# Delta heads: row broadcasts of the queries' decays issued behind the replicated reads of the diagonal blocks

## The chip, the core and the metric

The kernel runs on one core of a Trainium2 chip. The metric is the time on the device in microseconds (us), from the core's first to its last instruction and what lies around that; the median of the runs is compared. A core has a matrix engine (TensorE, in the profile PE, with its weight loads as PEld), VectorE (DVE), ScalarE (ACT), GpSimd (POOL) and SyncE (SP), which here issues all DMAs. Each engine works through its own list of instructions in order, and waits on semaphores for the others and for DMAs.

## The reference

One inference step of a small diffusion backbone of two layers, for a prompt of 128 tokens and a latent sequence of 1024, both with 1024 features. Layer 0 mixes a gated linear recurrence with windowed attention, layer 1 is a bidirectional gated DeltaNet with 8 heads; each layer ends in a SwiGLU network. The change lies in the DeltaNet. Cut to what matters, for one head and one direction, with chunks of tokens:

```python
decay = exp(where(incl, gc[:, None] - gc[None, :], NEG))       # gc: running sum of g in a chunk
a_mat = where(strict, beta[:, None] * kk * decay, 0.0) + eye(C)
sol   = triangular_solve(a_mat, concat([v * beta, k * (beta * exp(gc))]))   # u, w
qk    = (q @ k.T) * decay
qg    = q * exp(gc)[:, None]
for each chunk, in order:                                      # S starts from the context's state
    v_new = u - w @ S
    o     = qg @ S + qk @ v_new
    S     = S * exp(gc[-1]) + kd.T @ v_new
```

`exp(gc)` of the last factor of `qg` is what the moved DMAs bring: one number for each token, needed by every one of the 128 features. The outputs are the two sequences, the keys and values, and the final states of the recurrences.

## The kernel before

The 1152 tokens (9 blocks of 128) lie along the free dimension, features along the 128 partitions. The DeltaNet stage (`delta_stage`) takes the 8 heads one after another; for all engines but TensorE the heads 1 to 6 are a hardware loop (`heads`), and the first and the last head are written apart. Nothing but the order of the lines decides the order of the work: each engine's function lists its instructions, and semaphores tie the engines together. In the traced execution the stage runs from about 1615 to 2838 us.

One head goes as follows. TensorE projects v and z (`tile`), and in the scan the next head's k and q (`ahead`); VectorE and ScalarE convolve and normalise. `blocks_of` (lines 2441 to 2450, VectorE) makes the strictly triangular matrices of both directions, and by a reduction (L2448) the 16 x 16 blocks on their diagonals, `dn.part[d]`. The inverse of these blocks is found by substitution (`substitute`, L1797), for which each partition needs the block's rows in its own free dimension. SyncE brings them there through DRAM: two copies of `dn.part[d]` into `blocks_dram` (`blocks_spill` in the trace, L1869), a wait until they have landed (`a_out`), and one read that spreads each of the 16 rows there over 8 partitions, `dn.rep[d]` (L1871, the replicated read). VectorE substitutes direction 0, GpSimd direction 1; `expand` (L1815) then writes the inverses of the blocks into full matrices, `tt[0]` (`dn_tt`) and `tt[1]` (which lies in the buffer of `osum`, the previous head's output). TensorE transposes them (`turn_of`, L2107) and builds the full inverse from 16 to 128 in three levels (`x_of`, `d_of`, L2119 to L2137), with masked blocks that GpSimd makes (`masked`). Then come the solution, and the scan over the blocks in both directions.

SyncE's function (`body`, from L1854) lists for each head, in this order: the two loads of the states; the two row broadcasts of `exp(gc)` into `dn.qg[d]` (`rows`, L1847: 128 partitions x 9 blocks x 128 numbers from `rows_dram`, `rows_spill` in the trace); the copies and replicated reads of both directions; the store of the previous head's output to `y_dram` (`y_spill`, L1877); the loads of weight panels, each behind a wait for a split of GpSimd; the next head's broadcasts for the decay matrix; and the stores of the final states. The head starts when TensorE has issued the last output of the previous one (`o_full`). All these DMAs go through one queue, q1 of the profile.

`dn.qg[d]` is read by GpSimd's `decayed_q(d)`, which waits for the states and both broadcasts (`s_loaded` at 64 a head) and stands behind the second masked block of direction 1. The store of `osum` is waited for (`y_stored`) by VectorE, before it expands direction 1 into that buffer, and by ScalarE before the first output.

Of the kernel before, what the change touches and what calls it, by code (L numbers as in the profile page):

```python
# [1732 lines left out]
def delta_stage(s, dn, back):  # L1733
# [11 lines left out]
    with ExitStack() as ctx:  # L1745
        def sem(name):
            return ctx.enter_context(nc.semaphore("dn_" + name))
# [16 lines left out]
        s_loaded, ws_full, vn_ready, sn_full, s_ready, o_full, o_act, o_dve = (  # L1764
            sem(n) for n in ("s_loaded", "ws_full", "vn_ready", "sn_full", "s_ready", "o_full", "o_act", "o_dve"))
# [8 lines left out]
        def by_block(t):  # L1774
            return t[:].rearrange("p (n w) -> p n w", w=P)
# [51 lines left out]
        def heads(eng, body):  # L1827

            body(0, True, True)
            with eng.Fori(1, LAST) as h:  # L1830
                body(h, False, True)
            body(LAST, False, False)
# [5 lines left out]
        @block.sync  # L1838
        def _(sp):
            def load(h, j):  # L1840
                s.sp_load(sp, 4 * h + (p0 + j), (p0 + j) % 2)

            by_head = s.rows_dram.rearrange("q (n h) c -> q h n c", h=DN_H)

            def rows(h, q, to):

                return sp.dma_start(by_block(to), by_head[q, ds(h, 1)].to_broadcast([P, NT, P]))  # L1847

            sp.sem_inc(fin_stored, 32)
            sp.sem_inc(y_stored, 16)  # L1850
            for d in range(2):
                rows(0, d, dn.rows[d]).then_inc(rows_full, 16)
            for j in range(2, 6):
                load(0, j)  # L1854

            def body(h, first, more):
                if not first:
                    sp.wait_ge(o_full, 17 * h)
                for d in range(2):
                    sp.dma_start(dn.state[d][0][:], I["state_delta"][d, ds(h, 1)].rearrange("a p n -> p (a n)")  # L1860
                                 ).then_inc(s_loaded, 16)
                for d in range(2):
                    rows(h, 2 + d, dn.qg[d]).then_inc(s_loaded, 16)

                for d in range(2):
                    sp.wait_ge(wt_ready, 6 * h + (3 * d + 2))
                    copies = s.blocks_dram[d].rearrange("(b r) (m x) -> r b m x", r=2, m=BASE)
                    for r in range(2):
                        sp.dma_start(copies[r], dn.part[d][:].rearrange("p n c -> p (n c)")).then_inc(a_out[d], 16)  # L1869
                    sp.wait_ge(a_out[d], 32 * h + 32)  # L1870
                    sp.dma_start(dn.rep[d][:].rearrange("p m n c -> p (m n c)"),  # L1871
                                 s.blocks_dram[d].rearrange("b (o x) -> b o x", o=1
                                                            ).to_broadcast([2 * NK, BASE // 2, NT * BASE * BASE])
                                 ).then_inc(rep_full[d], 16)
                if not first:
                    sp.wait_ge(y_done, h)
                    sp.dma_start(s.y_dram[:, ds(h - 1, 1), :].rearrange("p a t -> p (a t)"), dn.osum[:]  # L1877
                                 ).then_inc(y_stored, 16)
                if more:
                    load(h, 6)  # L1880
                    load(h, 7)
                    sp.wait_ge(qg_ready, 2 * h + 2)
                    sp.wait_ge(u_full, 2 * h + 2)
                    for d in range(2):
                        rows(h + 1, d, dn.rows[d]).then_inc(rows_full, 16)
                else:

                    sp.wait_ge(s.panel_used.sem, p0 + 4 * DN_H)
                    sp.wait_ge(y_stored, 16 * DN_H)
                    sp.dma_start(s.hl[:, 0:LAST, :].bitcast(F32), s.y_dram).then_inc(back.landed, 16)  # L1890
                sp.wait_ge(fin_ready, 2 * h + 2)
                for d in range(2):
                    sp.dma_start(s.O["delta"][ds(h, 1), d].rearrange("a p n -> p (a n)"), dn.fin[d]
                                 ).then_inc(fin_stored, 16)
                if more:
                    load(h, 8)
                    load(h, 9)
            heads(sp, body)
            sp.wait_ge(fin_stored, 32 * DN_H + 32)

# [826 lines left out]
```

## Time and profile before

| what | value |
|---|---|
| median of the runs | 3823.32 us (3822.99 to 3826.45, 3 runs) |
| the profiled execution | 3837.11 us, span 3835.3 us |
| TensorE busy | 3357.6 us, 88% of the span |
| VectorE, ScalarE, GpSimd busy | 50%, 27%, 30% |
| granted clock of TensorE, mean | 0.942 of full speed |
| queue q1 | 103372 packets, 234.82 MB, 19.6% of the 16 engines' span |

The table is an average over stages with different limits: the projections and the SwiGLU networks keep TensorE full, while in the DeltaNet heads the engines wait for one another. What a wait is worth is read in its own stage. In the rows below, a timeline's columns are the start in us, the duration in us, the engine, the line of the kernel, the operation and its tiles, the count, and in brackets the engine's idle time before it and what ended that. For a DMA the duration is that of its issue; when it landed is in a view of its own.

### The profile page before, as it was taken

The page shows a single profiled execution, that of the slowest core. Times are in us where ns is not written, and L with a number is a line of the kernel's source. Part 1 is how long each engine was busy: PE and PEld are TensorE (multiplying, and loading weights), DVE is VectorE, ACT ScalarE, POOL GpSimd, SP SyncE. Part 2 cuts the span into 40 slices and gives each one's busy share as a digit, 9 for nine tenths or more (in the row PEclk, how much of TensorE's full clock was granted, in tenths as well). Part 3 has the DMA queues.
Part 4 walks back from the last instruction along what each step waited for, and adds up shares of the span by engine and source line. Part 5 has one row for each costly group of instructions (what it writes and reads, how often), then busy time and mean ns, then how long its engine had stood idle before and what let it go on. Part 6 is the DMA issues. An engine that isn't in the chain of part 4 may idle for free. (4 is left out here: it accounts for less than half of the span.)

```text
span 3835.3 us, 51814 instructions
## 1 busy us (share of the span) xinstructions
PE 3357.6 (88%) x20310; PEld 3203.7 (84%) x20310; DVE 1925.0 (50%) x2759; ACT 1031.7 (27%) x1573; POOL 1139.3 (30%) x797
## 2 busy tenths in 40 slices
PE   3984799899999999588888789788888999999996
PEld 2972589799999999478778778788788999999995
DVE  8758654734433445655465554655646132222227
ACT  3227340311111111343333433433422211111110
POOL 2213001321221112263554535535532212112121
PEclk8987799999999999799999899899999999999998
DMA  4420101212112211231221221222310111111111
GB/s 162 181 98 8 57 7 39 88 69 80 66 61 77 73 67 61 74 71 41 61 64 30 64 71 31 65 56 47 98 74 32 39 45 44 40 44 45 39 45 66
DMA packets 103577, 237.92 MB, mean 62 GB/s; under 512 B 8108, under 2 KB 61132, under 8 KB 100428
## 3 DMA queue, kind: packets, MB, share of 16 engines
q1 hardware_dynamic: 103372, 234.82, 19.6%
q8 instruction: 173, 2.83, 0.3%
q14 instruction: 32, 0.26, 0.0%
HBM read 217.54 MB, written 17.26 MB: 61 GB/s over the span
## 5 line engine op out<-in xcount | busy, mean ns | idle before, releaser
L55 PE MATMUL psum<-h_high,panel_high 128*128 128x384 f32 x3624 | 1246.0, 344 | 113.1 <-DVE h_low L495 81.1
L56 PE MATMUL psum<-h_low,panel_high 128*128 128x384 f32 x3624 | 1223.9, 338 | 0.0
L57 PE MATMUL psum<-h_high,panel_low 128*128 128x384 f32 x3624 | 1223.1, 337 | 0.0
L187 POOL TENSOR_TENSOR panel_low<-panel_raw,panel_high 128x1024 fp32r<-128x1024 f32 x196 | 488.0, 2490 | 1716.2 <-ACT panel_high L182 1673.4
L55 PEld LDWEIGHTS psum<-h_high,panel_high 128*128 128x128 f32 x3624 | 690.9, 191 | 154.4 <-issue 92.9
L56 PEld LDWEIGHTS psum<-h_low,panel_high 128*128 128x128 f32 x3624 | 691.5, 191 | 0.0
L57 PEld LDWEIGHTS psum<-h_high,panel_low 128*128 128x128 f32 x3624 | 690.0, 190 | 0.0
L847 DVE TENSOR_TENSOR ffn_product<-ffn_silu_gate,psum 128x1152 f32<-128x1152 f32 x44 | 59.6, 1354 | 712.4 <-PE psum L57 711.1
L182 ACT ACTIVATE panel_high<-panel_raw 128x1024 fp32r<-128x1024 f32 x195 | 205.1, 1052 | 627.6 <-PE psum L57 560.5
L55 PE MATMUL psum<-ffn_mid_high,panel_high 128*128 128x384 f32 x1056 | 355.2, 336 | 12.5 <-DVE x L650 7.5
L57 PE MATMUL psum<-ffn_mid_high,panel_low 128*128 128x384 f32 x1056 | 354.3, 336 | 0.0
L56 PE MATMUL psum<-ffn_mid_low,panel_high 128*128 128x384 f32 x1056 | 354.1, 335 | 0.0
L647 DVE SCALAR_TENSOR_TENSOR x<-psum,mod,x 128x128 f32<-128x128 f32 x192 | 67.3, 350 | 318.2 <-PE psum L57 306.8
L55 PEld LDWEIGHTS psum<-ffn_mid_high,panel_high 128*128 128x128 f32 x1056 | 199.4, 189 | 16.2 <-DVE x L650 8.8
L56 PEld LDWEIGHTS psum<-ffn_mid_low,panel_high 128*128 128x128 f32 x1056 | 199.2, 189 | 0.0
L57 PEld LDWEIGHTS psum<-ffn_mid_high,panel_low 128*128 128x128 f32 x1056 | 199.2, 189 | 0.0
L650 DVE SCALAR_TENSOR_TENSOR x<-psum,mod,x 128x768 f32<-128x768 f32 x192 | 193.5, 1008 | 0.0
L236 DVE CUSTOM_DVE_ANT_0 psum<-ffn_mod_panels,ffn_cond_rows 128x1024 f32<-128x1024 f32 x96 | 143.0, 1490 | 98.8 <-DMA ffn_mod_panels<-in_wmod 95.0
L772 ACT ACTIVATE ffn_mid_high<-ffn_product 128x1152 fp32r<-128x1152 f32 x44 | 51.5, 1169 | 512.1 <-DVE ffn_product L847 512.1
L769 ACT ACTIVATE ffn_silu_gate<-psum 128x1152 f32<-128x1152 f32 x44 | 49.9, 1135 | 439.5 <-PE psum L57 439.5
L236 DVE CUSTOM_DVE_ANT_0 psum<-in_mod_panels,in_cond_rows 128x1024 f32<-128x1024 f32 x64 | 99.0, 1547 | 47.7 <-DMA in_mod_panels<-in_wmod 44.9
L2307 ACT ACTIVATE dn_raw_k<-psum 128x384 f32<-128x384 f32 x144 | 70.3, 488 | 102.6 <-PE psum L2119 102.6
(320 smaller groups left out, 4740.5 us busy)
## 6 DMA issues: line engine op xcount, KB each, us to landing
panel_raw<-in_stream SPq DMA_DIRECT2D x197, 512.0 KB, 3.3
ffn_mod_panels<-in_wmod SPq DMA_DIRECT2D x24, 1024.0 KB, 7.3
dn_rep<-blocks_spill SPq DMA_DIRECT2D x16, 1152.0 KB, 7.7
in_mod_panels<-in_wmod SPq DMA_DIRECT2D x16, 1024.0 KB, 5.8
dn_qg<-rows_spill SPq DMA_DIRECT2D x16, 576.0 KB, 14.4
first_mod_panels<-in_wmod SPq DMA_DIRECT2D x8, 1024.0 KB, 14.0
x<-in_x SPq DMA_DIRECT2D x3, 1536.0 KB, 14.3
x<-in_x SPq DMA_DIRECT2D x1, 4608.0 KB, 15.9
```

What stands on the lines that cost most here:

```text
L55: pe.matmul(out, wh, xh, start=first, stop=False)
L56: pe.matmul(out, wh, xl, start=False, stop=False)
L57: return pe.matmul(out, wl, xh, start=False, stop=last)
L182: act.activation(self.wh[buf][:], self.raw[buf][:], ACT.Copy).then_inc(self.split_high.sem, 1)
L187: pool.tensor_tensor(self.wl[buf][:], self.raw[buf][:], self.wh[buf][:].bitcast(F32), ALU.subtract).then_inc(self.split_low.sem, 1)
L236: s.nc.vector.tensor_tensor_reduce(out=s.psum[:, 6:8, :], in0=panels[:, a, :].rearrange("p (b w) -> p b w", b=2), in1=rows[:, m, :].rearra ...
L647: dve.scalar_tensor_tensor(xf[:, 0:TP], s.psum[:, b0, 0:TP], g[0], xf[:, 0:TP], ALU.mult, ALU.add)
L650: return dve.scalar_tensor_tensor(later, s.psum[:, b0 + 1:b0 + 3, 0:TW], g[1], later, ALU.mult, ALU.add)
L769: act.activation(tiled(silu[:]), banks(s, 0), ACT.Silu).then_inc(s.gate_ready.sem, 1)
L772: act.activation(mid_h[slot][:], prod[:], ACT.Copy).then_inc(s.mid_high.sem, 1)
L847: dve.tensor_tensor(tiled(prod[:]), tiled(silu[:]), banks(s, 1), ALU.mult).then_inc(s.prod_ready.sem, 1)
L2307: act.activation(dn.xl[n % 2], psum[:, 6 + use % 2, 0:TW], ACT.Copy).then_inc(xb_read, 1)
```

## The change

The two lines that issue the row broadcasts move, within one head, from behind the state loads to behind the second replicated read, ahead of the store of the previous head's output. What is transferred, the semaphores and all waits stay.

```diff
--- before.py
+++ after.py
@@ -1860,9 +1860,6 @@
                     sp.dma_start(dn.state[d][0][:], I["state_delta"][d, ds(h, 1)].rearrange("a p n -> p (a n)")
                                  ).then_inc(s_loaded, 16)
                 for d in range(2):
-                    rows(h, 2 + d, dn.qg[d]).then_inc(s_loaded, 16)
-
-                for d in range(2):
                     sp.wait_ge(wt_ready, 6 * h + (3 * d + 2))
                     copies = s.blocks_dram[d].rearrange("(b r) (m x) -> r b m x", r=2, m=BASE)
                     for r in range(2):
@@ -1872,6 +1869,8 @@
                                  s.blocks_dram[d].rearrange("b (o x) -> b o x", o=1
                                                             ).to_broadcast([2 * NK, BASE // 2, NT * BASE * BASE])
                                  ).then_inc(rep_full[d], 16)
+                for d in range(2):
+                    rows(h, 2 + d, dn.qg[d]).then_inc(s_loaded, 16)
                 if not first:
                     sp.wait_ge(y_done, h)
                     sp.dma_start(s.y_dram[:, ds(h - 1, 1), :].rearrange("p a t -> p (a t)"), dn.osum[:]
```

SyncE's list in the first head, with the lines taken out (-) and put in (+); line numbers behind the change are lower by three. `dn_part` are the diagonal blocks (6746 direction 0, 6747 direction 1), `dn_rep` their replicated form:

```order
 L1860 DMA dn_state_6750<-in_state_delta 128x128
+L1866 DMA blocks_spill<-dn_part_6746 8x16x144 x2
+L1868 DMA dn_rep_6734<-blocks_spill 128x1x2304
+L1866 DMA blocks_spill<-dn_part_6747 8x16x144 x2
+L1868 DMA dn_rep_6735<-blocks_spill 128x1x2304
 L1847 DMA dn_qg_6727<-rows_spill 128x9x128
 L1847 DMA dn_qg_6728<-rows_spill 128x9x128
-L1869 DMA blocks_spill<-dn_part_6746 8x16x144 x2
-L1871 DMA dn_rep_6734<-blocks_spill 128x1x2304
-L1869 DMA blocks_spill<-dn_part_6747 8x16x144 x2
-L1871 DMA dn_rep_6735<-blocks_spill 128x1x2304
```

The copies of direction 0 now follow the state loads directly, and the broadcasts stand between the second replicated read and the loads of weight panels. The first head has no store of an earlier output.

SyncE's list in the loop over the heads 1 to 6 before the change, from the first replicated read on, with the waits; `dn_osum` is the previous head's output:

```order
L1871 DMA dn_rep_6734<-blocks_spill 128x1x2304 [waits dn_a_out0]
L1866 REGISTER_ALU
L1869 DMA blocks_spill<-dn_part_6747 8x16x144 [waits dn_wt_ready]
L1869 DMA blocks_spill<-dn_part_6747 8x16x144
L1871 DMA dn_rep_6735<-blocks_spill 128x1x2304 [waits dn_a_out1]
L1877 ISA [waits dn_y_done]
L1877 DMA y_spill<-dn_osum 128x1152
```

The same place after it:

```order
L1868 DMA dn_rep_6734<-blocks_spill 128x1x2304 [waits dn_a_out0]
L1863 REGISTER_ALU
L1866 DMA blocks_spill<-dn_part_6747 8x16x144 [waits dn_wt_ready]
L1866 DMA blocks_spill<-dn_part_6747 8x16x144
L1868 DMA dn_rep_6735<-blocks_spill 128x1x2304 [waits dn_a_out1]
L1847 ISA
L1847 DMA dn_qg_6727<-rows_spill 128x9x128
L1847 ISA
L1847 DMA dn_qg_6728<-rows_spill 128x9x128
L1876 ISA [waits dn_y_done]
L1876 DMA y_spill<-dn_osum 128x1152
```

The store of the output came directly behind the second replicated read; now the two broadcasts are issued between them. The waits in front of the copies, the reads and the store are the same.

## Rows read from the trace of the kernel before

**Rows 1.** Which engine waited for what, delta stage, 1640 to 2830 us.

```profile
engine line waited for: us in total, times, longest us
POOL dn_inverse L1803 <- DMA dn_rep<-blocks_spill: 119.3, 8, 17.0
PE psum L2107 <- DVE dn_tt L1818: 79.3, 8, 11.7
DVE dn_inverse L1803 <- DMA dn_rep<-blocks_spill: 73.5, 8, 9.8
```

**Rows 2.** Timeline of TensorE, end of the third head's projection and first transposes.

```profile
start us, us, engine line op out<-in xcount [idle before <-releaser]
...
1985.75 0.34 PE L57 MATMUL psum<-h_high,panel_low 128*128 128x384 f32 x1
1995.47 2.45 PE L2107 MATMUL psum<-ident,dn_tt 128*128 128x128 f32 x9 [9.38 <-DVE dn_tt L1818]
```

**Rows 3.** Timeline of VectorE in the third head (same columns).

```profile
...
1973.93 2.54 DVE L2434 RECIPROCAL dn_kd<-dn_kd 96x384 f32<-96x384 f32 x1
1985.64 0.31 DVE L1803 TENSOR_TENSOR dn_inverse<-dn_unit_blocks 128x144 f32<-128x144 f32 x1 [9.17 <-DMA dn_rep<-blocks_spill]
...
1994.05 1.36 DVE L1818 TENSOR_TENSOR dn_tt<-dn_inverse,dn_diagonal_blocks 128x1152 f32<-128x1152 f32 x1
...
2011.19 1.35 DVE L1818 TENSOR_TENSOR dn_osum<-dn_inverse,dn_diagonal_blocks 128x1152 f32<-128x1152 f32 x1
```

**Rows 4.** Timeline of SyncE in the third head (same columns); SPq issues DMAs.

```profile
...
1958.65 0.85 SPq L1860 DMA_DIRECT2D dn_state<-in_state_delta  x2
1959.70 1.34 SPq L1847 DMA_DIRECT2D dn_qg<-rows_spill  x2
1966.41 3.57 SPq L1869 DMA_DIRECT2D blocks_spill<-dn_part  x2
1978.01 0.58 SPq L1871 DMA_DIRECT2D dn_rep<-blocks_spill  x1
1978.71 1.21 SPq L1869 DMA_DIRECT2D blocks_spill<-dn_part  x2
1986.51 0.57 SPq L1871 DMA_DIRECT2D dn_rep<-blocks_spill  x1
1987.29 0.42 SPq L1877 DMA_DIRECT2D y_spill<-dn_osum  x1
...
2108.68 0.86 SPq L1860 DMA_DIRECT2D dn_state<-in_state_delta  x2
```

**Rows 5.** DMA issues, single broadcasts first, then medians of the stage.

```profile
issues: line engine op xcount, KB each, median us to landing
dn_qg<-rows_spill SPq DMA_DIRECT2D x1, 576.0 KB, 11.6
dn_qg<-rows_spill SPq DMA_DIRECT2D x1, 576.0 KB, 17.1
...
dn_rep<-blocks_spill SPq DMA_DIRECT2D x16, 1152.0 KB, 7.7
y_spill<-dn_osum SPq DMA_DIRECT2D x7, 576.0 KB, 8.2
dn_state<-in_state_delta SPq DMA_DIRECT2D x16, 64.0 KB, 2.8
```

**Rows 6.** Rate that the DMAs moved, 1958 to 1998 us in 40 slices.

```profile
...
GB/s 70 332 221 126 80 74 68 59 35 70 66 72 89 89 83 79 81 143 126 36 0 147 295 249 194 258 86 98 0 101 221 258 203 240 171 300 277 0 0 0
```

**Rows 7.** Timeline of SyncE at the end of the decay stage.

```profile
1611.51 0.39 SPq L1597 DMA_DIRECT2D rows_spill<-decay_rows_of_sums  x1
1614.23 0.41 SPq L1847 DMA_DIRECT2D dn_qn<-rows_spill  x1
```

**Rows 8.** Timeline of GpSimd in the third head.

```profile
...
1994.26 1.44 POOL L1803 TENSOR_TENSOR dn_inverse<-dn_unit_blocks 128x144 f32<-128x144 f32 x1 [14.69 <-DMA dn_rep<-blocks_spill]
...
2014.16 2.64 POOL L1906 TENSOR_TENSOR dn_qg<-dn_qn,dn_qg 128x1152 f32<-128x1152 f32 x1
```

**Rows 9.** Busy time by stretch, third head; PEclk is the granted clock.

```profile
core 0: us, PE busy (x) PEld busy (x) DVE busy (x) ACT busy (x) POOL busy (x), PEclk, DMA share, GB/s
1982.00:1986.00 4.00, 4.00 (x24) 3.77 (x22) 0.33 (x2) 0.00 (x0) 0.00 (x0) 1.00 0.72 159
1994.00:1998.00 4.00, 2.50 (x10) 1.99 (x11) 2.65 (x3) 1.03 (x3) 3.35 (x6) 0.50 0.17 69
1998.00:2002.00 4.00, 4.00 (x24) 4.00 (x24) 0.00 (x0) 1.43 (x3) 3.37 (x9) 0.62 0.00 0
```

## The prediction

> **What bounds the kernel now.** I read the waits of the delta stage first (1640 to 2830 us), then one head of it (the third, 1958 to 2109 us) on the matrix engine, VectorE, SyncE and GpSimd, then the landing times of its DMAs. The eight heads run one behind another, so what one head loses is lost eight times. In [rows 1] TensorE waits 79.3 us in eight times for `dn_tt` of line 1818: the expanded inverse of the diagonal blocks of direction 0. VectorE, which makes that tile, in turn waits 73.5 us in eight times for the replicated blocks, `dn_rep`. [rows 2] is that wait in the third head: the last matmul of the projection starts at 1985.75 and the transposes at 1995.47, 9.38 us idle. [rows 3] shows why: VectorE ended its reciprocal at 1976.47 (1973.93 + 2.54), stood 9.17 us, and only at 1985.64 began the substitution, which with the expansion ends at 1995.41 (1994.05 + 1.36). No other engine's work lies in the gap, so a microsecond by which the blocks come earlier is a microsecond off the head, until VectorE's 9.17 us or TensorE's 9.38 us are used up.
>
> Where the blocks are late is in [rows 4]. SyncE issues the two copies of direction 0 to DRAM from 1966.41 (the second issue alone ends at 1969.98) and can issue the replicated read only at 1978.01: 11.60 us. The two row broadcasts were issued at 1959.70, ahead of them on the same queue. By [rows 5] they land 11.6 and 17.1 us after their issues (1959.70 and 1960.26), so the second at 1977.36; the copies are in 0.65 us behind it. The copies wait for the broadcasts. [rows 6] is the rate that the DMAs moved, in slices of 1 us: after the loads at its start it stays between 35 and 89 GB/s in the 5th to 17th slice, while the first replicated read, in the 22nd to 28th, makes up to 295. The broadcasts are the slow piece on the queue.
>
> **The change part by part.** Nothing is added or removed; SyncE issues the two broadcasts behind the second replicated read instead of behind the state loads. Instruction counts stay. Call the first copy's issue T (1966.41 in this head); T hangs on VectorE's reduction, which the change doesn't touch.
>
> 1. *The copies of direction 0 find an empty queue.* The loads before them are in by T: the states were issued at 1958.65 and land in 2.8 us. No copy on an empty queue stands in the trace. The nearest row is the store of the sums of the decay stage, 144 KB as the two copies are together: issued at 1611.51, and SyncE, which waits for it, goes on at 1614.23, 2.72 us [rows 7]. The second copy is issued 0.6 us behind the first, as the pair of direction 1 is (1.21 us for both [rows 4]), so both are in at T + 3.3. From below, the state load's 2.8 us [rows 5] in place of the 2.72 gives T + 3.4, no less; I know nothing that would make it shorter than some 3. From above, the pair of direction 1 went from 1978.71 to 1986.51, 7.8 us, but behind a replicated read of 7.7 us. I take 3.3, which is the row of the same kind: gain 11.6 - 3.3 = 8.3 us a head, at worst 11.6 - 7.8 = 3.8.
>
> 2. *The first replicated read.* It keeps its 7.7 us: before, too, nothing slow was on the queue by then. It lands at T + 11.0 = 1977.4, behind VectorE's reciprocal (1976.47), so VectorE doesn't clip the gain. The expansion ends 8.3 us earlier, at 1987.1, behind the end of the projection (1986.1), so TensorE still waits 1.0 us and the whole 8.3 us count.
>
> 3. *Direction 1.* Its copies were issued as soon as the first read was, and landed just behind that read (0.8 us); that stays. So its read is issued at T + 11.8 instead of T + 20.1, lands at T + 19.5, and GpSimd begins its substitution 8.3 us earlier (1994.26 before [rows 8]). The distance between the two directions stays.
>
> 4. *The broadcasts themselves.* They are issued at about T + 12.5, behind the second read. Their reader is GpSimd's `decayed_q`, at 2014.16 before [rows 8], T + 47.8; moved up with the head, T + 39.5. If their flow starts at issue, they land as before, 17.7 us behind the first issue, T + 30.2; if nothing of them starts before the second read is in, T + 19.5 + 17.7 = T + 37.2. Either is before T + 39.5. Cost: nothing, hidden by the masked blocks that GpSimd makes in between; without that cover each late microsecond would hold GpSimd's next masks.
>
> 5. *The store of the previous head's output* (`y_spill`, seven heads) now stands behind the broadcasts. Before, it was issued at 1987.29 and landed 8.2 us later, 1.3 us behind the read that was issued at 1986.51 and took 7.7 [rows 4, 5]. As far behind the broadcasts it would be in at T + 31.5 or, at the late end, T + 38.5. VectorE waits for it before it overwrites `osum` in the second expansion, at 2011.19 before [rows 3], T + 44.8; moved up, T + 36.5. So it costs between nothing and 2.0 us in each of seven heads. I take nothing: the 35 to 89 GB/s of [rows 6] leave most of the rate that the read shows unused, so that the broadcasts can start beside it; the other end stays in the range. The panel loads behind the store are issued only when GpSimd has split a panel, past T + 36, with the queue clear or nearly so.
>
> 6. *TensorE's clock.* [rows 9]: the granted clock is 1.00 (2.4 GHz) while the projection runs (1982 to 1986), 0.50 (1.2 GHz) in 1994 to 1998 after the 9.38 us of idling, and still 0.62 in 1998 to 2002. With 1.0 us of idling it may not fall. Bounds: nothing, or half of the 6.5 us from the first transposes to 2002, some 3 us; ScalarE's copies pace these steps too, so I take 0.5 us a head.
>
> Sum: 8 x (8.3 + 0.5) = 70 us of the profiled execution's 3837.1 (its span is 3835.3, the rest lies around it). That is 1.8%. On the median of the runs, 3823.3, which is 0.36% below the profiled one, 1.8% is 69 us, and the forecast 3754.
>
> A rule of the Trainium skill speaks against this. Its page "DMA: Bandwidth & Descriptors", section "Anatomy of one DMA", prices a DMA at about 2.0 us plus its bytes over 436 GB/s. By that the two broadcasts would be through in about 2.0 + 2 x 1.35 = 4.7 us (an estimate from that page), before the copies are issued, and the change would be worth nothing; the trace has 17.1 us for the second, so I go by the trace and keep the rule's result as the case of no effect.
>
> **The rivals.**
>
> *The copies are slow by themselves.* Then the queue in front of them is not what they wait for, and clearing it brings little. For it: the pair of direction 1, with no broadcast in front, also needs 7.8 us. Against: that pair lands 0.8 us behind the read ahead of it, the pair of direction 0 lands 0.65 us behind the second broadcast, and the store of the same size takes 2.72 us. At 7.8 us a pair the gain is 8 x 3.8 = 30 us: 3793. At the 11.6 us of now it is nothing: 3823, and the change would not do what it says.
>
> *The change buys the wait back at the output's store.* This is the case on the other side. If the broadcasts begin only when the second read is in (T + 19.5), need 17.7 us, and the store is then taken up with 8.2 us of its own, it lands at T + 45.4, 8.9 us behind VectorE's need at T + 36.5. Seven heads lose 62 us and eight gain 70: 3815. Each further microsecond costs 7 us, so from a store at T + 46.6 on the kernel is slower, and a store at T + 48.5 ends at 3837. For it: VectorE does wait for the store in every head but the first, and the store is put behind the slowest transfer on the queue. Against: the store landed 1.3 us behind the transfer ahead of it, not 8.2. The milder form, 2.0 us in seven heads, gives 3768.
>
> *More than forecast.* If the copies are quicker still and the clock stays up, VectorE's 9.2 us and 1.5 us of clock come back in each head: 86 us, 3738.
>
> **How the numbers follow.** Forecast, with the store at most 2 us late (3745 to 3770): 0.68. More than that: 0.08. Copies slow in part, or the store late by several microseconds (3770 to 3815): 0.17. No effect: 0.04. Store past the break-even: 0.03. The range 3738 to 3792 leaves out the far half of the slow copies, no effect, slower, and a little of "more": about 0.18. 0.2% is 7.6 us, about what a measurement here can tell from no change: faster 0.93, same 0.04, slower 0.03.
>
> **What would show it.** In the profile after: SyncE's wait for the copies for direction 0 (1969.98 to 1978.01) falls from 8.0 to some 2.3 us, with the issue of its pair down from 3.57 to 1.2, and stays for direction 1; VectorE's wait for `dn_rep` falls from 73.5 to about 9 us; TensorE's for the expansion from 79.3 to about 15; GpSimd's for `dn_rep` (119.3 us) falls by some 60; the broadcasts' median landing rises above 14.4; the store lands some 18 to 25 us after its issue, with no wait for it on VectorE; one head takes about 141 us instead of 150.0 (1958.65 to 2108.68, state load to state load [rows 4]). The forecast is wrong if the copies still need over 6 us, if VectorE idles before the second expansion, or if GpSimd stops at `decayed_q`.

## The result, and the profile after

| | before | after |
|---|---|---|
| median of the runs | 3824.82 us (3822.99 to 3826.45, 4 runs) | 3778.94 us (3775.33 to 3782.22, 4 runs) |
| the profiled execution | 3837.11 us, span 3835.3 | 3779.03 us, span 3777.3 |

The ratio of the times is 0.9872 (95% interval 0.9859 to 0.9884): 46 us faster, where 69 were forecast. The change was measured twice more beside the experiments: 3772.19 us against 3828.55, ratio 0.9862 (0.9846 to 0.9879), and 3773.31 against 3831.89, ratio 0.9853 (0.9839 to 0.9866), gains of 56 and 59 us. The two profiled executions are 58 us apart, so a sum over the traces has to come to 58, where the prediction's came to 70.

The first step of the change did what it was to do. SyncE in the third head after, as in [rows 4] (the kernel's line numbers are now lower by one to three):

```profile
start us, us, engine line op out<-in xcount [idle before <-releaser]
1949.45 1.26 SPq L1866 DMA_DIRECT2D blocks_spill<-dn_part  x2
1952.53 0.58 SPq L1868 DMA_DIRECT2D dn_rep<-blocks_spill  x1
1954.22 1.22 SPq L1866 DMA_DIRECT2D blocks_spill<-dn_part  x2
1960.64 0.57 SPq L1868 DMA_DIRECT2D dn_rep<-blocks_spill  x1
1961.42 1.51 SPq L1847 DMA_DIRECT2D dn_qg<-rows_spill  x2
1963.12 7.63 SPq L1876 DMA_DIRECT2D y_spill<-dn_osum  x1
```

From the first copy to the replicated read it is 3.08 us (1949.45 to 1952.53) instead of 11.60, and the copies' issue takes 1.26 instead of 3.57. The store of the output is now the piece that stands behind the broadcasts: its issue alone takes 7.63 us. The landings in the delta stage, as in [rows 5]:

```profile
issues: line engine op xcount, KB each, median us to landing
dn_rep<-blocks_spill SPq DMA_DIRECT2D x16, 1152.0 KB, 7.7
...
dn_qg<-rows_spill SPq DMA_DIRECT2D x16, 576.0 KB, 15.4
...
y_spill<-dn_osum SPq DMA_DIRECT2D x7, 576.0 KB, 18.8
...
```

The replicated read kept its 7.7 us, the broadcasts take 15.4, the store 18.8 instead of 8.2. The waits of the stage (1640 to 2790 us), the lines that answer to [rows 1], and one more:

```profile
engine line waited for: us in total, times, longest us
...
POOL dn_inverse L1803 <- DMA dn_rep<-blocks_spill: 52.5, 8, 9.5
...
PE psum L2106 <- DVE dn_tt L1818: 35.9, 8, 5.5
...
PE psum L2106 <- DVE dn_osum L1818: 12.4, 8, 2.6
...
DVE dn_inverse L1803 <- DMA dn_rep<-blocks_spill: 6.7, 8, 2.0
```

VectorE's wait for the blocks fell from 73.5 to 6.7 us, by 8.4 a head. But TensorE's wait for what VectorE makes of them fell only from 79.3 to 35.9, not to the 15 that were forecast. The difference, some 20 us, is lost between the blocks' landing and the end of the expansion, on VectorE itself. VectorE in the third head, which answers to [rows 3]:

```profile
1951.99 2.20 DVE L2447 TENSOR_REDUCE dn_part<-dn_ub 128x144 f32<-128x1152 f32 x1
...
1956.96 2.54 DVE L2433 RECIPROCAL dn_kd<-dn_kd 96x384 f32<-96x384 f32 x1
1960.13 2.62 DVE L1803 TENSOR_TENSOR dn_inverse<-dn_unit_blocks 128x144 f32<-128x144 f32 x1 [0.63 <-DMA dn_rep<-blocks_spill]
1962.79 0.30 DVE L1809 TENSOR_TENSOR dn_part<-dn_rep,dn_inverse 128x135 f32<-128x135 f32 x1
...
1968.38 0.22 DVE L1812 TENSOR_TENSOR dn_inverse<-dn_inverse,dn_part 128x54 f32<-128x54 f32 x1
1968.63 0.34 DVE L1809 TENSOR_TENSOR dn_part<-dn_rep,dn_inverse 128x45 f32<-128x45 f32 x1
1969.00 0.47 DVE L1812 TENSOR_TENSOR dn_inverse<-dn_inverse,dn_part 128x45 f32<-128x45 f32 x1
...
1972.34 1.42 DVE L1818 TENSOR_TENSOR dn_tt<-dn_inverse,dn_diagonal_blocks 128x1152 f32<-128x1152 f32 x1
...
1988.17 0.56 DVE L2499 TENSOR_TENSOR dn_t<-dn_t,psum 128x384 f32<-128x384 f32 x1 [0.99 <-PE psum L2136]
1988.64 0.55 DVE L2500 TENSOR_TENSOR dn_tt<-dn_tt,psum 128x384 f32<-128x384 f32 x1
1989.10 1.97 DVE L1818 TENSOR_TENSOR dn_osum<-dn_inverse,dn_diagonal_blocks 128x1152 f32<-128x1152 f32 x1
```

And GpSimd beside it, as in [rows 8]:

```profile
1959.93 2.65 POOL L1905 TENSOR_TENSOR dn_osum<-dn_osum,dn_silu_z 128x1152 f32<-128x1152 f32 x1
1968.48 0.42 POOL L1803 TENSOR_TENSOR dn_inverse<-dn_unit_blocks 128x144 f32<-128x144 f32 x1 [5.90 <-DMA dn_rep<-blocks_spill]
...
1987.23 2.63 POOL L1905 TENSOR_TENSOR dn_qg<-dn_qn,dn_qg 128x1152 f32<-128x1152 f32 x1
```

Two places are to be seen. The first instruction of VectorE's substitution takes 2.62 us instead of 0.31. It reads the constant unit blocks, so no data can be late for it; what runs beside it is GpSimd's multiply of the previous head's output with its gate (`gated`, 128 x 1152), from 1959.93 to 1962.58, and VectorE goes on at 1962.79. Then, from 1968.48, GpSimd's substitution of direction 1 has started, and VectorE's steps go from 0.22 to 0.34 and 0.47 us. From the start of the substitution to the end of the expansion VectorE took 9.77 us before (1985.64 to 1995.41 [rows 3]) and takes 13.63 now (1960.13 to 1973.76). The second expansion, at 1989.10, takes 1.97 us instead of 1.35 [rows 3], beside a `decayed_q` (1987.23 to 1989.86). The two additions ahead of it, which ran beside the same `decayed_q` and take one of their inputs from the matrix engine's result memory (`psum`), kept their 0.56 and 0.55 us (0.55 also at 2015.50, where GpSimd idles): not every VectorE instruction is held. In the first head, which has no previous output to gate, the same instruction still takes 0.31 us:

```profile
1676.62 0.31 DVE L1803 TENSOR_TENSOR dn_inverse<-dn_unit_blocks 128x144 f32<-128x144 f32 x1 [2.04 <-DMA dn_rep<-blocks_spill]
```

All heads can be set beside one another by counting from the issue of the first copy (T of the prediction) to the start of later steps. Means over heads 2 to 8 in us, worked out from VectorE's and SyncE's timelines of each kernel (the last column, T to T of the next head, over heads 2 to 7):

| kernel | substitution | expand, dir. 0 | expand, dir. 1 | first update of the solution, dir. 1 | product qk | one head |
|---|---|---|---|---|---|---|
| before | 19.3 | 27.7 | 44.8 | 53.8 | 78.5 | 150.2 |
| after | 10.7 | 22.6 | 39.2 | 49.6 | 71.6 | 143.2 |
| gate on 8 columns | 10.7 | 19.1 | 34.6 | 45.6 | 69.2 | 140.9 |
| one broadcast in front | 12.0 | 21.7 | 38.1 | 47.8 | 71.7 | 143.6 |
| three masks later | 10.7 | 19.1 | 37.5 | 47.8 | 71.8 | 143.9 |
| two masks later | 10.8 | 19.9 | 36.3 | 45.8 | 71.2 | 143.0 |
| two later, store first | 10.7 | 19.9 | 35.2 | 44.4 | 70.8 | 142.9 |
| before, gate held to the blocks | 19.2 | 31.1 | 48.4 | 57.9 | 79.5 | 151.3 |
| gate on VectorE | 11.5 | 20.1 | 35.7 | 46.0 | 69.1 | 141.0 |
| two later, `decayed_q` on 8 columns | 10.8 | 19.8 | 35.0 | 44.1 | 67.7 | 139.7 |

The gain at each mark, after against before: 8.6 when the substitution starts, 5.1 at the expansion, 5.6 at that of direction 1, 4.2 at the first update, 6.9 at the product, 7.1 at the head's end. The first head alone, without the gate, gained 9.2 (150.8 to 141.6).

### The profile page after: what moved, and what is told of

Its sections match the earlier page's. It is cut to its first block and busy times, and to the rows that moved or that the text cites. A ratio compares the mean times of both kernels' runs of the same rounds, so it can differ in the third digit from the quotient of the medians.

```text
span 3777.3 us, 51814 instructions
## 1 busy us (share of the span) xinstructions
PE 3345.6 (89%) x20310; PEld 3189.6 (84%) x20310; DVE 1943.7 (51%) x2759; ACT 1030.9 (27%) x1573; POOL 1125.7 (30%) x797
## 3 DMA queue, kind: packets, MB, share of 16 engines
q1 hardware_dynamic: 103372, 234.82, 19.9%
## 6 DMA issues: line engine op xcount, KB each, us to landing
dn_qg<-rows_spill SPq DMA_DIRECT2D x16, 576.0 KB, 15.4
```

## The experiments

Before the runs the shortfall had several candidates. Theory A: VectorE's substitution has been moved under GpSimd's gate multiply, and is held by it. Theory B: it is the incoming DMA traffic that slows VectorE's instruction. Other rivals are the store of the output behind the broadcasts, the queue, and what GpSimd and VectorE do to each other later in the head. Ratios are against the kernel before, run on the same chip.

**The gate's multiply on 8 of its 1152 columns.**

```diff
-                    mul(dn.osum[:], dn.osum[:], dn.silu_z[:]).then_inc(y_done, 1)
+                    mul(dn.osum[:, 0:8], dn.osum[:, 0:8], dn.silu_z[:, 0:8]).then_inc(y_done, 1)
```

> The changed kernel, but GpSimd's gate of the previous head's output (gated) multiplies 8 of the 1152 columns only, so it leaves out most of that product. Theory A (VectorE and GpSimd keep each other out: the first instruction of the substitution, which does not even read the replicated blocks, runs 2.6 us instead of 0.31 because GpSimd's gate is running, and then the two substitutions overlap): that instruction falls back to 0.31 us in all heads, substitution and expansion from 13.6 to about 9.8 us, TensorE's wait for the expansion from 36 to about 10 us, and the time to about 3755 (3779 less 7 heads x some 3.5 us). Theory B (the incoming traffic, copies and read of direction 1, slows VectorE's work on the SBUF): nothing in the traffic changes, so the instruction stays at 2.6 us and the time at 3779, within 4.

Measured: 3759.13 us, ratio 0.9824 (0.9803 to 0.9846), 66 us faster than before. GpSimd and VectorE in the third head:

```profile
1953.21 0.27 POOL L1905 TENSOR_TENSOR dn_osum<-dn_osum,dn_silu_z 128x8 f32<-128x8 f32 x1
1961.70 1.44 POOL L1803 TENSOR_TENSOR dn_inverse<-dn_unit_blocks 128x144 f32<-128x144 f32 x1 [8.23 <-DMA dn_rep<-blocks_spill]
```

```profile
1953.10 0.31 DVE L1803 TENSOR_TENSOR dn_inverse<-dn_unit_blocks 128x144 f32<-128x144 f32 x1 [0.33 <-DMA dn_rep<-blocks_spill]
```

The 0.31 us are back, and the expansion stands at T + 19.1, where the forecast had it (8.6 ahead of before). TensorE's wait for it is 12.1 us in eight times. That is what theory A said; by B nothing should have changed, as the traffic is the same. The run also lightens GpSimd by 2.4 us a head, but not where it counts: behind the gate GpSimd waits for the blocks of direction 1 in any case, 5.90 us after the change and 8.23 here (third head).

**One broadcast in front, one behind.** This undoes half of the change.

```diff
+                rows(h, 2, dn.qg[0]).then_inc(s_loaded, 16)
                 for d in range(2):
...
-                for d in range(2):
-                    rows(h, 2 + d, dn.qg[d]).then_inc(s_loaded, 16)
+                rows(h, 3, dn.qg[1]).then_inc(s_loaded, 16)
```

> The changed kernel with the broadcast of direction 0 back in front of the copies and that of direction 1 behind the second read. Both theories: the first read is issued some 2.9 us later than in the changed kernel, about T + 6.0 (the broadcast lands 11.6 us after its issue). Queue alone, with nothing lost on VectorE: 8 x 2.9 = 23 us slower than the changed kernel, about 3802. Theory A: the substitution then begins at about T + 13.7, just behind the end of the gate at T + 13.1, runs its 9.8 us without GpSimd, and the expansion ends at T + 23.5 instead of T + 24.3; only the first head, which has no gate, loses 2.9 us: 3772 to 3782, no slower than the changed kernel.

Measured: 3778.13 us, ratio 0.9877 (0.9861 to 0.9894). In the third head the copies need 4.31 us with one broadcast ahead of them (6.0 were expected), and the substitution starts at T + 12.0 on the mean, 1.3 us later than after the change. Yet the expansion is 0.9 us earlier: the first instruction, started later under the same multiply, takes less, 1.24 us on the median of the eight heads instead of 2.66. The later start cost nothing, because the gate would have held the substitution for that time anyway.

**The last three masked blocks of direction 0 behind GpSimd's substitution**, so that the gate runs earlier and is over when the blocks come.

```diff
-                for c in range(RING + NB):
+                for c in range(RING):
                     masked(0, c)
...
-                for c in range(RING + NB, SLOTS):
+                for c in range(RING, SLOTS):
```

> The changed kernel with GpSimd's masked blocks 5 to 7 of direction 0 made behind its substitution instead of ahead of the gate; everything is computed. The gate then runs from about T + 7.9 to T + 10.5 and is over when the blocks land at T + 10.7. Theory A: the first instruction of the substitution takes 0.31 us, the expansion ends some 3.8 us earlier in seven heads, the masks come just in time (TensorE wants block 5 at about T + 33, it is ready at about T + 32.5): 3755 to 3762. If the masks are late: up to 2 us a head of it lost again, 3770. Theory B: no change, 3779 within 4.

Measured: 3781.79 us, ratio 0.9882 (0.9859 to 0.9904): no gain over the change, and the expectation missed. The collision is gone (VectorE's first instruction is 0.31 us again, the expansion at T + 19.1), but a new wait has come, for the masked blocks themselves:

```profile
engine line waited for: us in total, times, longest us
...
PE psum L2118 <- POOL dn_vf L1905: 16.3, 8, 2.8
PE psum L2106 <- DVE dn_tt L1818: 13.4, 8, 3.6
```

TensorE waits 16.3 us for blocks that GpSimd now makes too late. The gain of 3.5 us at the first expansion is 1.7 at the second and nothing at the product.

**The store of the output ahead of the broadcasts.**

```diff
-                for d in range(2):
-                    rows(h, 2 + d, dn.qg[d]).then_inc(s_loaded, 16)
                 if not first:
...
+                for d in range(2):
+                    rows(h, 2 + d, dn.qg[d]).then_inc(s_loaded, 16)
```

> The changed kernel with the store of the previous head's output issued ahead of the two broadcasts. The store lands some 8 to 9 us after its issue instead of 18.8, the broadcasts a little later. If the late store costs nothing, as the profile of the changed kernel says (nobody waits for it in seven heads): 3779, within 4. If part of the shortfall of the forecast is the store's: up to 14 us faster, 3765.

Measured: 3773.49 us, ratio 0.9864 (0.9848 to 0.988); the change's own 0.9872 lies within that interval. The store is not where the gain went.

**Two masked blocks later instead of three** (the ranges end at `RING + 1`), beside the change itself, run again.

> The changed kernel with GpSimd's masked blocks 6 and 7 of direction 0 (not 5) made behind its substitution; everything is computed. The gate ends at about T + 11.4 instead of T + 13.1, so the first instruction of VectorE's substitution at T + 10.7 is held some 0.7 us instead of 2.5. Block 5 is there early, block 6 is ready 0.9 us behind the substitution and wanted 2 us after block 5. Theory A: TensorE's wait for the expansion falls from 36 to about 20 us, no wait for masks as in the run with three masks moved (16.3 us there): 10 to 20 us faster than the changed kernel, about 3764. If the masks still come late, or what is gained here is lost again at the second expansion: 3775 to 3782.

> The changed kernel once more, unedited, on the same chip and beside the same runs of the kernel before, so that the edits of this set are compared with it: 3779, within 5 us.

Measured: 3772.70 us, ratio 0.9855 (0.9839 to 0.9872), against 3772.19, 0.9862 (0.9846 to 0.9879), for the change: no difference, where a gain was expected. The change itself, run again, missed its expectation of 3779 within 5 us by 2 us. The waits for masks are small now, the expansion is 2.7 us earlier and the first update in direction 1 3.8, but at the product 0.4 is left. The lead is given back in the direction-1 phase, between the update and the product: 25.4 us against 22.0 after the change (and 24.7 before it). In that phase VectorE convolves v, while GpSimd makes masked blocks and the two `decayed_q` products. VectorE's instructions of that convolution sum, over the eight heads, to 84.9 us here, 68.3 after the change and 79.3 before. The means hide two kinds of heads: in heads 2 to 4 the update comes at T + 44.0 to 44.3 and the convolution of the head takes 10.3 to 13.1 us; in heads 5 to 8 it comes at T + 46.8 to 47.3 and the convolution takes 9.0 to 9.9.

**The kernel before, with the gate held until the blocks have landed.** This puts the collision into the kernel that has none of the change.

```diff
                 if not first:
+                    pool.wait_ge(rep_full[0], 16 * h + 16)
                     gated(h)
```

> The kernel before, with one wait more on GpSimd: the gate of the previous head's output starts only when the replicated blocks of direction 0 have landed, that is at the very moment at which VectorE starts its substitution. GpSimd idles there anyway (14.3 us a head until the blocks of direction 1 land), and the order of the DMAs is that of before. Theory A: the first instruction of the substitution takes 2.6 to 2.9 us instead of 0.31 in seven heads, and the time rises by some 7 x 2.4 = 17 us, to about 3842. If the slow instruction in the changed kernel came from its DMA traffic (B), or if it costs nothing in the end: the time of before, 3825, within 4.

Measured: 3840.09 us, ratio 1.0032 (1.002 to 1.0043): 12 us slower than before, where 17 were expected. VectorE and GpSimd in the third head:

```profile
1986.47 0.31 DVE L1803 TENSOR_TENSOR dn_inverse<-dn_unit_blocks 128x144 f32<-128x144 f32 x1 [8.49 <-DMA dn_rep<-blocks_spill]
1986.82 2.61 DVE L1809 TENSOR_TENSOR dn_part<-dn_rep,dn_inverse 128x135 f32<-128x135 f32 x1
1989.46 0.30 DVE L1812 TENSOR_TENSOR dn_inverse<-dn_inverse,dn_part 128x135 f32<-128x135 f32 x1
```

```profile
1986.60 2.67 POOL L1906 TENSOR_TENSOR dn_osum<-dn_osum,dn_silu_z 128x1152 f32<-128x1152 f32 x1 [8.13 <-DMA dn_rep<-blocks_spill]
```

VectorE's first instruction started ahead of the multiply and takes its 0.31 us; the second one started behind it and takes 2.61, until the multiply ends at 1989.27. So it is not the one instruction, its data or the DMAs: of the substitution, the instruction that starts while the multiply runs is held to about its end. The change run again shows it unedited: in its third and eighth head the gate happened to start 0.21 and 0.03 us behind the first instruction, and the second took 2.64 and 2.65 us. The expansion is 3.4 us later than before, as it is later in the change than in the run with the narrow gate (3.5). Of that 1.0 us is left at the head's end; the rest is given back in the direction-1 phase (21.6 us instead of 24.7). The 1.0 is of one trace and no sharper than its heads: the first head, which has no gate, took 147.5 us here and 150.8 before.

**Two masks later and the store first, together.** (Both edits as above.)

> The run with two masks later, with the store of the previous head's output ahead of the broadcasts as well. The store alone gave 3773.5 against 3779, less than the runs of one kernel differ; if that was real: some 5 us below the run with two masks later, about 3759; if not, the same.

Measured: 3773.41 us, ratio 0.9864 (0.9847 to 0.988), the time of the run with two masks later. Again the update comes earlier (T + 44.4), and again the product doesn't (70.8). VectorE's two longest instructions in between, in the third head, and GpSimd's beside them:

```profile
1992.04 3.09 DVE L2411 TENSOR_SCALAR dn_vf<-dn_raw_v,dn_conv 128x1152 f32<-128x1152 f32 x1
...
2002.61 3.32 DVE L2418 SCALAR_TENSOR_TENSOR dn_vf<-dn_raw_v,dn_conv,dn_vf 128x1023 f32<-128x1023 f32 x1
```

```profile
1991.88 2.63 POOL L1905 TENSOR_TENSOR dn_qg<-dn_qn,dn_qg 128x1152 f32<-128x1152 f32 x1
...
2002.50 2.35 POOL L187 TENSOR_TENSOR panel_low<-panel_raw,panel_high 128x1024 fp32r<-128x1024 f32 x1
```

The first of these started just behind a `decayed_q` (1991.88 to 1994.51) and ended 0.6 us after it; the second began 0.11 us after GpSimd's panel split and outlived it. That the neighbour holds them too is a reading of these times and not tested by itself.

**The gate on VectorE.** The multiply moves to VectorE, behind the norm of the previous output, where VectorE stood waiting for the blocks before the change.

```diff
-                if not first:
-                    gated(h)
                 substitute(pool, 1, h)
...
                     norm_o(h)
+                    dve.wait_ge(post_step, 2 * h)
+                    dve.tensor_tensor(dn.osum[:], dn.osum[:], dn.silu_z[:], ALU.mult).then_inc(y_done, 1)
```

> The changed kernel with the gate of the previous head's output on VectorE, directly behind its norm (heads 1 to 7), instead of on GpSimd; everything is computed. It costs VectorE about 1.35 us ahead of the reciprocal, which then ends at about T + 11.4 instead of T + 10.1, 0.7 us behind the landing of the blocks. GpSimd's masks are over by T + 10.5, so the substitution isn't held (0.31 us for its first instruction), and the expansion ends at about T + 21 instead of T + 24: by the front of the head alone 15 to 20 us faster than the changed kernel, 3752 to 3760. But the runs with masks moved showed a second toll behind it: the part of the head up to the product of the decay with qk ended at T + 71.5 whatever the front gained, with VectorE's convolution of v and GpSimd's work for direction 1 colliding. If that holds here too: 3765 to 3775.

> The changed kernel, unedited, beside these three on the same chip: 3775, within 6 us.

Measured: 3754.69 us (3751.44 to 3760.7, 5 runs), ratio 0.9799 (0.9785 to 0.9812), against 0.9853 (0.9839 to 0.9866) for the change in the same set. The intervals don't meet: this version beats both kernels. VectorE in the third head:

```profile
1952.99 1.50 DVE L2486 TENSOR_TENSOR dn_osum<-dn_osum,dn_silu_z 128x1152 f32<-128x1152 f32 x1
1954.41 2.54 DVE L2431 RECIPROCAL dn_kd<-dn_kd 96x384 f32<-96x384 f32 x1
1956.87 0.31 DVE L1803 TENSOR_TENSOR dn_inverse<-dn_unit_blocks 128x144 f32<-128x144 f32 x1
```

The multiply takes 1.50 us on VectorE (2.65 on GpSimd), delays the substitution by 0.8 us, and takes away the 2.3 us of holding. One head is 9.2 us shorter than before.

**The same, with the store first.** (The edits of both.)

> The run with the gate on VectorE, with the store of the previous head's output ahead of the broadcasts as well. The store brought nothing measurable in two runs; I expect the time of the run with the gate on VectorE, within 5 us.

Measured: 3756.12 us, ratio 0.9803 (0.9788 to 0.9818), as without. The store's place doesn't matter here either.

**Two masks later, and `decayed_q` on 8 of 1152 columns**, to see what gave the lead back.

```diff
-                    mul(dn.qg[d][:], dn.qn[:], dn.qg[d][:]).then_inc(qg_ready, 1)
+                    mul(dn.qg[d][:, 0:8], dn.qn[:, 0:8], dn.qg[d][:, 0:8]).then_inc(qg_ready, 1)
```

> The run with two masks later, but GpSimd's two products of q with its decays (decayed_q) take 8 of the 1152 columns only, so most of that product is left out; GpSimd has some 5 us a head less to do while VectorE convolves v. If the second toll is the collision of that convolution with GpSimd's work: the product of the decay with qk comes at about T + 67 to T + 69 instead of T + 71.5, and the time falls by 16 to 32 us from 3773, to 3741 to 3757. If what holds that point is something else (ScalarE's copies, TensorE): 3773 within 5, and T + 71.5.

Measured: 3747.55 us, ratio 0.9783 (0.9769 to 0.9796), against 0.9855 for the two masks alone. The product is now at T + 67.7 (71.2 without). ScalarE's wait for the convolved v in the two runs, first with the whole `decayed_q`, then on 8 columns:

```profile
ACT dn_vf L2250 <- DVE dn_vf L2418: 37.9, 8, 5.2
```

```profile
ACT dn_vf L2250 <- DVE dn_vf L2418: 20.3, 8, 3.0
```

So with less of GpSimd's work in the direction-1 phase the lead stays: of the 3.5 us by which the product comes earlier, 1.7 stand at the first update already and 1.8 come behind it. Which way isn't settled: the convolution's instructions still sum to 86.0 us (84.9 with the whole products), so none of it shows there. Being held at a worse moment and GpSimd's being late by itself aren't told apart by this run.

## Why the prediction was right, and where its size was off

*Steps 1 and 2, up to the landing: right.* The copies take 3.08 us on the empty queue (3.3 forecast), the replicated read 7.7, and the substitution starts at T + 10.7 instead of 19.3: 8.6 us a head, where 8.3 were counted. "The copies are slow by themselves" is out, and so is the case of no effect. The price behind that case, in the Trainium skill's page "DMA: Bandwidth & Descriptors", section "Anatomy of one DMA", is stated there for DMAs that GpSimd issues. SyncE issues these broadcasts, and the trace has 15.4 us for them at the median; the measurement decides.

*Step 2, its last sentence: this is the term that was mis-sized.* "The expansion ends 8.3 us earlier" took VectorE's stretch from the blocks to the end of the expansion to keep its length. It went from 9.77 to 13.63 us in the third head, so that the expansion started 5.1 us earlier on the mean and not 8.3. The cause is shown from both sides: with the gate shrunk or moved the first instruction is 0.31 us again, and with the gate pushed onto the blocks in the kernel before, an instruction of 0.30 us takes 2.61. It could have been read beforehand: in [rows 8] GpSimd has idled for 14.69 us when it starts its substitution at 1994.26, so it was busy until 1979.57, and the prediction's own 1977.4 for the landing lies 2.2 us inside that. The line of the kernel before is:

```profile
1976.90 2.67 POOL L1906 TENSOR_TENSOR dn_osum<-dn_osum,dn_silu_z 128x1152 f32<-128x1152 f32 x1
```

"No other engine's work lies in the gap" was right as far as data goes; but the engine beside it was working there, and that cost was put at nothing without a reason.

The Trainium skill states the rule for it: its page "SBUF — State Buffer", section "Who interferes with whom", says that a VectorE instruction with two inputs in SBUF (the on-chip memory in which the tiles lie) contends with a GpSimd instruction that reads SBUF, and that the ports they share are an exclusive lock. The 2.62 us in place of 0.31, and the 2.61 of the held gate, agree with it, and so do the additions with one input in `psum`, which kept their time.

*Step 3: GpSimd's start came earlier as forecast* (T + 19.0 in the third head; T + 19.5 was forecast). The copies of direction 1 no longer follow the first read at once: they wait for VectorE's reduction of direction 1, which ends at 1954.19, and are issued at 1954.22, 1.1 us behind the end of that read's issue. It costs nothing, as their own read is issued at T + 11.2 (T + 11.8 forecast). The distance between the two reads stayed (8.1 us, 8.5 before), but VectorE's work slid towards GpSimd's: GpSimd begins at 1968.48, while VectorE, held, comes to its eleventh pair of steps. The steps that overlap take up to 0.51 us, and with the 2.3 of the first they make up nearly all of the 3.9. After that the loss goes on: from the second expansion to the first update of direction 1 the gain falls from 5.6 to 4.2 us. Then 2.7 come back by the product, which no step of the prediction had: VectorE's convolution of v takes 68.3 us in all instead of 79.3, 1.4 us a head. The table shows it as a pattern: from the first update to the product it takes 22.0 us after the change and 21.6 in the kernel before with the gate held, the two rows with the whole collision, and 23.1 to 26.4 in every other row. So the collision costs 3.5 us at the expansion, and behind it some of that comes back later in the head; why the convolution then runs shorter is not shown.

*Steps 4 and 5: right.* `decayed_q` starts at 1987.23 with no idle time before it. The store's place costs nothing, as three pairs of runs show, and in the trace after VectorE waits for no store. The rival on the slower side is out.

*Step 6, the clock: its condition didn't come.* In the third head TensorE still idles 4.54 us ahead of the transposes, and its granted clock falls as it did in [rows 9]; with the gate's multiply on 8 columns it idles 0.57 us. After the change, and in that run:

```profile
1973.82 2.45 PE L2106 MATMUL psum<-ident,dn_tt 128*128 128x128 f32 x9 [4.54 <-DVE dn_tt L1818]
```

```profile
1962.92 0.88 PE L2106 MATMUL psum<-ident,dn_tt 128*128 128x128 f32 x6 [0.57 <-DVE dn_tt L1818]
```

```profile
core 0: us, PE busy (x) PEld busy (x) DVE busy (x) ACT busy (x) POOL busy (x), PEclk, DMA share, GB/s
...
1973.00:1977.00 4.00, 3.15 (x13) 2.65 (x14) 2.02 (x2) 1.47 (x3) 3.45 (x8) 0.50 0.32 79
1977.00:1981.00 4.00, 4.00 (x32) 4.00 (x31) 0.87 (x2) 1.10 (x3) 3.14 (x12) 0.82 0.54 185
```

```profile
core 0: us, PE busy (x) PEld busy (x) DVE busy (x) ACT busy (x) POOL busy (x), PEclk, DMA share, GB/s
1958.00:1962.00 4.00, 4.00 (x23) 4.00 (x24) 3.48 (x16) 0.00 (x0) 0.30 (x1) 1.00 0.98 207
1962.00:1966.00 4.00, 3.09 (x23) 2.42 (x22) 2.12 (x2) 2.97 (x5) 3.53 (x7) 1.00 0.31 74
```

In that head the clock stays at 1.00 (2.4 GHz) in the one run and falls to 0.50 (1.2 GHz) in the other. Over the heads of the run on 8 columns it stays at 1.00 in the five where TensorE idles 0.56 to 1.47 us there, and falls in the three where it idles 2.10 to 3.69; after the change it falls in all eight (3.53 to 5.53 us). With the gate on VectorE it stayed at 1.00 behind 2.12 us as well, so these rows give no sharp limit. The argument was right, and the collision cost this term too.

*The sum.* In the traces, head by head: the first gained 9.2 us (8.8 forecast), the next six 7.1 on the mean. 9.2 + 6 x 7.1 = 52 of the 58, the rest in the last head and behind it. With the gate shrunk the whole comes to 66 us of medians (3825.57 to 3759.13), with the gate on VectorE to 77 (3831.89 to 3754.69), on either side of the 69 forecast; a head of theirs is 9.3 and 9.2 us shorter than before, where 8.8 were forecast. So with the multiply out of the way a head gains about what the sum had. How much of the 66 and 77 is the collision at the front alone, and how much later collisions, isn't split further. The stated range held the result, but by luck as far as the cause goes: 3779 lies in the stretch (3770 to 3815) that the prediction had kept for slow copies or a late store, and neither came. Why the three comparisons of the change span 46 to 59 us stays open.

## What to carry to other kernels

Where one order on a queue holds a small transfer behind a slow one, read the distance between issue and landing and move the slow one behind; the slow one's own reader says how far. Then ask of the work that comes earlier what runs on the neighbouring engine at its new time, not only what it waits for: a time read from an old place on the timeline holds only there. And where an engine that sits idle can do the neighbour's instruction, moving that instruction may be worth more than moving its time.

## What the runs showed of the hardware

- A VectorE instruction with both inputs in SBUF, 0.30 us by itself, takes until about the end of a GpSimd multiply of 128 x 1152 that started shortly before it: 2.61 and 2.62 us, at either of two instructions. Additions with one input in `psum`, beside such a multiply, kept their 0.55 us.
- Two copies of 72 KB each took 3.08 us with an empty queue, 4.31 with one broadcast issued 6.7 us ahead (3.3 to 5.7 over the heads), 11.60 with two.
- The issue of the store took 7.63 us on SyncE right behind two broadcasts, 0.88 behind one, in the third head.
- The same multiply, 128 x 1152 in float32, takes 2.65 us on GpSimd and 1.50 on VectorE.
